# Two more expert weight units in the first round, and the first norm's g and b spread on chip

## What is computed

```python
x = _layer_norm(DEEPNORM_ALPHA * x + mixed, ln1_g[l], ln1_b[l])
ffn = _hier_moe(x, router_group_w[l], ..., expert_w_gate[l], expert_w_up[l], expert_w_down[l])
x = _layer_norm(DEEPNORM_ALPHA * x + ffn, ln2_g[l], ln2_b[l])
```

```python
def _hier_moe(x, wg_r, bg_r, we_r, be_r, w_gate, w_up, w_down):
    ...
    h = jax.nn.silu(jnp.einsum('td,edf->etf', xt, w_gate)) * jnp.einsum('td,edf->etf', xt, w_up)
    h = h * combine.T[:, :, None].astype(h.dtype)
    return jnp.einsum('etf,efd->td', h, w_down).reshape(B, S, D)
```

## Time and profile before

| what | us |
| --- | --- |
| median of 3 runs | 1340.41 |
| lowest and highest run | 1337.76, 1341.34 |
| the profiled execution, its own time | 1338.06 |
| its span (first to last instruction) | 1335.7 |
| PE busy in the span | 1308.4 |
| DVE, ACT busy | 584.3, 483.6 |

### The profile page before, as it was taken

The page is one execution under the profiler, slowest core; times in us unless marked ns, Lnnn a source line. Parts: engine busy times, 40 slices in busy tenths (PEclk is TensorE's granted clock), DMA queues, the critical chain, the costliest instruction groups (busy, mean ns, idle before and its releaser), DMA issues.

```text
span 1335.7 us, 17769 instructions
## 1 busy us (share of the span) xinstructions
PE 1308.4 (98%) x7293; PEld 962.3 (72%) x7293; DVE 584.3 (44%) x757; ACT 483.6 (36%) x671; POOL 28.2 (2%) x49
## 2 busy tenths in 40 slices
PE   9999999999999999999999999999999999999995
PEld 8999989998888888888888888854454443544442
DVE  4387444546545555554455555525112121221207
ACT  4554344435465634454333433422121121211211
POOL 1000000400000000000100001000000000000000
PEclk9999999999999999999999999999999999999997
DMA  9767555545545445654556795799999999999995
GB/s 304 266 197 260 171 189 190 189 159 174 172 136 179 157 142 173 198 163 162 183 197 212 267 391 182 264 398 414 421 421 422 421 421 421 422 420 421 421 407 222
DMA packets 120749, 364.95 MB, mean 273 GB/s; under 512 B 11560, under 2 KB 17128, under 8 KB 96880
## 3 DMA queue, kind: packets, MB, share of 16 engines
q1 hardware_dynamic: 114368, 359.58, 72.6%
q10 hardware_dynamic: 6320, 4.49, 1.1%
HBM read 361.95 MB, written 2.10 MB: 273 GB/s over the span
## 4 chain that ended last, share of the span: by engine, by line
PE 91%; DMA 6%; DVE 1%; SPq 1%; issue 0%; ACT 0%; DVEq 0%
PE main L1142 19%; PE main L1144 19%; PE main L1143 19%; PE main L541 14%; PE att L614 7%; PE att L495 4%; DMA mraw<-in_expert_w_down_dram 3%; DMA mraw<-in_expert_w_up_dram 2%; PE att L1391 1%; SPq L396 1%; PE main L507 1%; PE main L508 1%; PE att L1374 1%; PE att L1410 1%; PE att L1406 1%; PE att L1361 0%
## 5 line engine op out<-in xcount | busy, mean ns | idle before, releaser
L1808 DVE TENSOR_TENSOR wlo<-raw,whi 128x2048 fp32r<-128x2048 f32 x134 | 308.1, 2299 | 352.7 <-ACT whi L1557 352.7
L1557 ACT ACTIVATE whi<-raw 128x2048 fp32r<-128x2048 f32 x134 | 256.1, 1911 | 412.0 <-PE main L1144 409.8
L541 PE MATMUL main<-mraw,xg 128*64 128x512 f32 x1024 | 225.2, 595 | 0.7 <-DMA mraw<-in_expert_w_up_dram 0.6
L1142 PE MATMUL main<-whi,xhi 128*128 128x512 f32 (+1 forms) x544 | 203.8, 375 | 0.0
L1144 PE MATMUL main<-whi,xlo 128*128 128x512 f32 (+1 forms) x544 | 201.7, 371 | 0.0
L1143 PE MATMUL main<-wlo,xhi 128*128 128x512 f32 (+1 forms) x544 | 201.5, 370 | 0.0
L541 PEld LDWEIGHTS main<-mraw,xg 128*64 128x64 f32 x1024 | 72.0, 137 | 136.6 <-issue 135.4
L1142 PE MATMUL main<-xhi,whi 128*128 128x256 f32 (+1 forms) x560 | 159.5, 285 | 1.0 <-DVE wlo L1940 1.0
L1143 PE MATMUL main<-xlo,whi 128*128 128x256 f32 (+1 forms) x560 | 158.4, 283 | 0.0
L1144 PE MATMUL main<-xhi,wlo 128*128 128x256 f32 (+1 forms) x560 | 158.4, 283 | 0.0
L1144 PEld LDWEIGHTS main<-whi,xlo 128*128 128x128 f32 x544 | 102.5, 188 | 17.7
(11 more groups left out here) (331 smaller groups left out, 1336.5 us busy)
## 6 DMA issues: line engine op xcount, KB each, us to landing
raw<-in_w_in_dram SPq DMA_DIRECT2D x95, 1024.0 KB, 5.1
mraw<-in_expert_w_gate_dram SPq DMA_DIRECT2D x64, 1024.0 KB, 21.5
mraw<-in_expert_w_up_dram SPq DMA_DIRECT2D x64, 1024.0 KB, 22.9
mraw<-in_expert_w_down_dram SPq DMA_DIRECT2D x62, 1024.0 KB, 21.3
raw<-in_w_branch_dram SPq DMA_DIRECT2D x24, 1024.0 KB, 5.1
raw<-in_w_out_dram SPq DMA_DIRECT2D x16, 1024.0 KB, 6.7
xin<-in_x_dram SPq DMA_DIRECT2D x4, 512.0 KB, 8.2
mraw<-in_expert_w_down_dram SPq DMA_DIRECT2D x4, 512.0 KB, 6.9
```

What stands on the lines that cost most here:

```text
L541: ins = pe.matmul(main[0][half, w, :], xg[:, k, half], src[:, kk * DE:(kk + 1) * DE], start=(k == 0), stop=(k == KT - 1))
L1142: pe.matmul(o, ah, bh, start=start, stop=False, skip_group_check=skip)
L1557: act.activation(whi[:, u % SPLIT, 0:n], raw[:, slot, 0:n], ACT.Copy).then_inc(hi_done, 1)
L1808: dve.tensor_tensor(wlo[:, u % SPLIT, 0:n], raw[:, slot, 0:n], whi[:, u % SPLIT, 0:n].bitcast(F32), ALU.subtract).then_inc(lo_done, 1)
```

## The change

**Places.** Places 20 and 21 (over `khT` and `qst`) become first places: `NP` is 22. A list `first` gives the place of each of the first 22 units: units 0 to 5 in places 0 to 5, units 6 and 7 in places 20 and 21, units 8 and 9 in places 14 and 15 (those under `out_acc`), and units 10 to 21 in the rest in order. The ring of 19 begins at unit 22. The load of units 6 and 7 is issued where `l1g` and `l1b` were loaded. Units 22 and 23 are the ones in halves.

**g and b.** `l1g` and `l1b` are gone. The 8 rows are loaded into the first 8 partitions of a new tile `rows` (128 x 512), which POOL sets to zero at the start; ACT scales them by ALPHA in place after their transposition. PE spreads a row over all partitions with a matmul of f32, 128 x 512, whose stationary operand is a column of the identity (`spread`, four for g, into the four banks of `att`). For b the spread opens the accumulation of each of the 8 scatter pieces of pair 0 (`with_b`).

**Order.** `start_sum` on DVE stands ahead of `gated`, and is eight products of `xr` with `att`. PE waits for `acc_ok` ahead of pair 0's down product; SP no longer does.

```diff
         places.append(made["sig"])
+        norm_places = (len(places), len(places) + 1)
+        places += [made["khT"], made["qst"]]
         NP = len(places)
-        places += [made["khT"], made["qst"]]
+        late = [once[0], once[1]]
+        first = [0, 1, 2, 3, 4, 5, *norm_places, *late, *(j for j in range(6, router_place + 1) if j not in late)]
         mraw = [at(f"mraw{j}", o, [P, UNIT]) for j, o in enumerate(places)]
-        second_round = [j for j in range(NP) if j not in once]
-        GROWN = NP + len(second_round)
-        ring = second_round[:4] + [NP, NP + 1] + second_round[4:]
+        ring = [j for j in first if j not in once]
         assert len(ring) == MRAW
 
         def place(g):
-            if g < NP:
-                return g
-            return second_round[g - NP] if g < GROWN else ring[(g - GROWN) % MRAW]
+            return first[g] if g < NP else ring[(g - NP) % MRAW]
 
         def user_before(g):
-            return max((e for e in range(g) if place(e) == place(g)), default=None)
-
-        LOOP0, LAST0 = (FIRST * MU - GROWN) % MRAW, (FIRST * MU + MU - GROWN) % MRAW
+            return max((e for e in range(g) if place(e) == place(g)))
+
+        LOOP0, LAST0 = (FIRST * MU - NP) % MRAW, (FIRST * MU + MU - NP) % MRAW
         L2R = MU - MRAW
         l2g, l2b, ysb = (at(n, places[ring[(LAST0 + L2R + j) % MRAW]], [P, D]) for j, n in enumerate(("l2g", "l2b", "ysb")))
...
@@ -400,21 +399,21 @@
             sp.dma_start(mraw[j][:, cols].unsqueeze(1), expert_unit(g % MU, g // MU)[:, :, cols]).then_inc(mlanded[j], 16)
 
         def first_units(sp, some):
-            for r in some:
-                if r < 4:
+            for j in some:
+                if j < 4:
                     sp.wait_ge(unit_used, U1)
-                elif r < 6:
+                elif j < 6:
...
                     sp.wait_ge(r_ps, T)
-                else:
-                    sp.wait_ge(unit_used, U1 + 4 * QUADS - (1 if r < 8 + RAW else 0))
-                load_unit(sp, r, 0, r)
+                elif j < router_place:
+                    sp.wait_ge(unit_used, U1 + 4 * QUADS - (1 if j < 8 + RAW else 0))
+                load_unit(sp, first.index(j), 0, j)
 
         def moe_loads(sp):
-            first_units(sp, range(6, NP))
...
@@ -422,10 +421,7 @@
                 sp.wait_ge(m_used, user_before(g) + 1)
                 load_half(sp, g, 1)
             for g in range(NP + 2, FIRST * MU):
-                if user_before(g) is None:
-                    sp.wait_ge(acc_ok, 1)
-                else:
-                    sp.wait_ge(m_used, user_before(g) + 1)
+                sp.wait_ge(m_used, user_before(g) + 1)
                 load_unit(sp, g % MU, g // MU, place(g))
             sp.wait_ge(np_ok, 1)
             turns = sp.value_load(runs[0:1, 0:1], min_val=1, max_val=1 + PAIRS * (PASSES - 1))
...
@@ -496,16 +492,22 @@
                                         start=(k % 4 == 0 and t == 0), stop=(t == 1), skip_group_check=True)
                 ins.then_inc(xg_ps, 1)
 
-            def scatter(c, before):
+            def spread(o, r):
+                return pe.matmul(o, ident[:, r:r + 1].to_broadcast([P, P]), rows[:], start=True,
+                                 stop=(r < QUADS), skip_group_check=True)
+
+            def scatter(c, before, with_b=False):
 
                 pe.wait_ge(y_lo, before * 4 + c + 1)
                 for t in range(T):
                     n = 2 * c + t
                     if n >= 2:
                         pe.wait_ge(sc_free, before * 8 + n)
-                    rows, o = wsl[:, t * P:(t + 1) * P], scattered(n)
-                    pe.matmul(o, rows, yhi[:, c % 2, :], start=True, stop=False)
-                    pe.matmul(o, rows, ylo[:, c % 2, :], start=False, stop=True).then_inc(sc_ps, 1)
+                    place_t, o = wsl[:, t * P:(t + 1) * P], scattered(n)
+                    if with_b:
+                        spread(o, QUADS + c)
+                    pe.matmul(o, place_t, yhi[:, c % 2, :], start=not with_b, stop=False, skip_group_check=with_b)
+                    pe.matmul(o, place_t, ylo[:, c % 2, :], start=False, stop=True, skip_group_check=with_b).then_inc(sc_ps, 1)
 
             def last_scatter(d, m):
 
...
@@ -530,6 +532,11 @@
 
                     pe.wait_ge(xg_out, 1 + q + m * 4)
                     for w in range(2):
+                        if fixed == 0 and q == 2 and w == 1:
+                            pe.wait_ge(xg_out, 4)
+                            pe.wait_ge(gb_out, 2)
+                            for r in range(QUADS):
+                                spread(att[:, r, :], r).then_inc(l1_in, 1)
                         for a in range(2):
                             _, landed_, value = unit(4 * q + 2 * w + a)
                             pe.wait_ge(landed_, value)
...
@@ -547,7 +554,7 @@
 
                 def put(c):
                     if fixed != 0:
-                        scatter(c, m - 1)
+                        scatter(c, m - 1, fixed == 1)
 
                 pe.wait_ge(hot_ok, 1 + m)
                 put(0)
@@ -602,6 +609,8 @@
                 for f in range(DE // P):
                     if f % 2 == 0:
                         pe.wait_ge(ht_out, 1 + f // 2 + m * 2)
+                    if fixed == 0 and f == 0:
+                        pe.wait_ge(acc_ok, 1)
                     for a in range(2):
                         _, landed_, value = unit(4 * QUADS + 2 * f + a)
                         pe.wait_ge(landed_, value)
...
@@ -859,29 +868,26 @@
                 dve.tensor_scalar(bag[:, :, 1], bag[:, :, 1], EPS, None, ALU.add).then_inc(l2_var, 1)
 
             def start_sum():
-                dve.wait_ge(m_used, once[1] + 1)
-                dve.wait_ge(l1_in, 32)
+                dve.wait_ge(m_used, first.index(late[1]) + 1)
                 dve.wait_ge(z_ok, T)
-                for t in range(T):
-                    for q in range(QUADS):
-                        cols = slice(q * 512, (q + 1) * 512)
-                        ins = dve.scalar_tensor_tensor(out_acc[:, t, cols].rearrange("p (m k) -> p m k", k=4),
-                                                       xr[:, t, cols].rearrange("p (k m) -> p m k", k=4), ALPHA,
-                                                       l1g[:, cols].rearrange("p (m k) -> p m k", k=4), ALU.mult, ALU.mult)
-                link(ins)
-                for t in range(T):
-                    ins = dve.scalar_tensor_tensor(out_acc[:, t, :], l1b[:], ALPHA, out_acc[:, t, :], ALU.mult, ALU.add)
+                for q in range(QUADS):
+                    cols = slice(q * 512, (q + 1) * 512)
+                    dve.wait_ge(l1_in, q + 1)
+                    for t in range(T):
+                        ins = dve.tensor_tensor(out_acc[:, t, cols].rearrange("p (m k) -> p m k", k=4),
+                                                xr[:, t, cols].rearrange("p (k m) -> p m k", k=4),
+                                                att[:, q, :].rearrange("p (m k) -> p m k", k=4), ALU.mult)
                 ins.then_inc(acc_ok, 1)
                 dve.wait_ge(acc_ok, 1)
 
-            def pair_step(m, first=False):
+            def pair_step(m, starts=False):
                 dve.wait_ge(ws_t, 1 + m)
                 slots((m + 1) % PAIRS, m + 2)
                 slot_weights((m + 1) % PAIRS, m + 2)
+                if starts:
+                    start_sum()
                 gated(m)
-                if first:
-                    start_sum()
-                else:
+                if not starts:
                     put_last(m - 1)
                 put(m)
 
...
@@ -1022,6 +1030,7 @@
                         load(u, u % RAW, src.rearrange("(k p) n -> p k n", p=P), 4, 512,
                              turn=u - RAW + 1 + i * UB)
             sp.wait_ge(att_free, 9)
+            sp.wait_ge(consts, N_CONST)
             for j, name in enumerate(("ln1_g", "ln1_b")):
                 sp.dma_start(gb[j * QUADS:(j + 1) * QUADS, :], A[name][0].rearrange("(q n) -> q n", n=512)).then_inc(gb_in, 16)
             for dst, name in ((wrg, "router_group_w"), (wre, "router_expert_w")):
@@ -1029,8 +1038,7 @@
                              A[name][0].rearrange("(q p k) n -> p q (k n)", p=P, k=4)).then_inc(wr_in, 16)
             sp.dma_start(br[:, 0:NG], A["router_group_b"].to_broadcast([P, NG])).then_inc(br_in, 16)
             sp.dma_start(br[:, NG:NG + NE], A["router_expert_b"].to_broadcast([P, NE])).then_inc(br_in, 16)
-            sp.dma_start(l1g[:], A["ln1_g"].to_broadcast([P, D])).then_inc(l1_in, 16)
-            sp.dma_start(l1b[:], A["ln1_b"].to_broadcast([P, D])).then_inc(l1_in, 16)
+            first_units(sp, norm_places)
             for c in range(4):
                 for q in range(QUADS):
                     u = U1 + c * QUADS + q
...
@@ -1074,7 +1082,7 @@
             pool.affine_select(out=rowok[:], in_=rowok[:], compare_op=ALU.is_ge, fill=0.0, base=1 - CMP,
```

(31 more changed lines are left out.)

## The result

The changed kernel takes 1344.70 us in the median of 6 runs (1343.82 to 1346.59), against 1340.01 for the kernel before in 6 runs beside it. The ratio is 1.0039 with a 95% interval of 1.0028 to 1.0049: slower, by about 5 us. The forecast was 1340.3 and no difference, range 1337.0 to 1343.8; the measured time lies outside it. Rival (c), a spread at 0.85 us and 1344.9 in all, is the nearest. The profiled execution took 1345.38 us. Two executions far from all others are left out of the medians: one of the kernel before (5153.42 us) and one of the experiment with g's spreads later (2244.17 us, granted clock 0.56).

The account below looks back on a forecast made before the run. The stream of expert units bounds the kernel, with PE close behind. From the profiled 1338.06 us, minus 4.5 gain plus 4.4 for later use of unit 24 gives 1338.0, or 1340.3 on the median's scale; range 1337.0 to 1343.8.

Parts of the forecast that it names:

- Rival (c): PE's added f32 spreads cost 0.85 us each, making PE 4.5 us late: 1344.9 us in all; chance 6%.
- twelve spreads of 0.44 us: Price of the added f32 128 x 512 matmuls on PE, read from nearest trace rows: 0.44 us each, 5.3 in all.
- what PE has more: Part pricing PE's added matmuls in pairs 0 and 1; ten of them make unit 24 used 4.4 us later.
- Unit 24 and the slack of 4.5 us: Unit 43's load waits for PE to use unit 24; its 4.5 us of slack caps the gain from two more places.
- The restart: A unit loaded into an empty queue, such as unit 43, lands 4.8 us after issue.
- The first hole: Units 30 and 31 wait for units 10 and 11; the stream stands still some 3 us, which does not decide.
- PE's own path: PE gets 5.3 us longer, but its 5.7 us of waits for the stream take that up.
- Work that costs nothing: Sum's start on DVE (5.5 to 8.8 us), later units 8 and 9, and ACT's and POOL's additions all stay hidden.
- (d): DVE's start of the sum comes late, holding PE and the stream; at 2.0 us a product, 1344.8 us; chance 4%.
- (e): Units 6 and 7 go out early but the stream, limited by `m_used`, is never ahead: 1340.4 to 1342 us; chance 3%.
- (a): Restarting the dry load stream costs up to 2.4 us more than taken: 1342.7 us; chance 12%.

## Why the prediction was wrong

**The step that failed** is the term "twelve spreads of 0.44 us" in the part on what PE has more. On PE's path they measured 3.80 us for the four of g (3.63 in their own chain row, 0.91 each) and 6.75 for the eight of b (0.84 each), 10.55 in all instead of 5.3. The reading of the nearest rows was wrong in two ways, and both could be seen in the document. First, the eight matmuls of the earlier trace rows (L1490) are transposes through the identity, which the program calls `pe.transpose`, and not products. Second, an f32 product is two rows of the trace: the program's order lists a gather as eight matmuls (`x8`), and the chain shows sixteen for it. The gather's row of the kernel before:

```profile
880.74 1.98 PE att L495 x16
```

So 1.98 us for sixteen rows is 0.25 us for a product of 128 columns, and 1.07 us for four rows of 256 columns is two products, 1.07 us for 512 columns. The expert products were misread in the same way: their 64 rows in 13.93 us are 32 matmuls of the program (eight units with four each, `gate_up`), so two that share the array take 0.87 us, not 0.44. I had counted the rows of the trace as if they were the program's. The count should have been made in the one place where both views show the same instruction.

The Trainium skill's page FP8 and Floating Point Precision (TensorE Precision Notes) says four passes for true FP32. The run bears it out: 0.86 us for a spread's two rows in the chain, at a granted clock of 1.00, is 4 x 512 columns at 2.4 GHz (0.853). The stationary operand's step of zero, the other reason that rival (c) named, is not needed for it: the gather's products have none and take 0.22 to 0.25 us for 128 columns, and the fp32r spreads have it and take 0.28. The prediction set the page against a row that was of another kind of instruction, and gave its case 6%.

**Unit 24 and the slack of 4.5 us: right in mechanism.** With the measured price unit 24 is late by 3.8 + 5.2 = 9.0 us (from 58.6 to 67.6 us behind the first product), less 4.5 is 4.5, and unit 43 landed 4.5 us later (72.45 against 67.96). The restart took 4.9 us, where 4.8 was read from the earlier trace rows. The rest of the loss at the last landing (5.8 us in the profiles), 1.3 us, arises behind unit 43. Pauses of the stream of over 0.3 us each add up to 2.7 us there, 2.1 in the kernel before, so they cover about half; what makes them stays open.

**The first hole: size off.** Forecast about 3 us; it was 6.0. The spreads of g took 3.8 instead of 1.8, and the restart there took 6.1 us from issue to landing, as in the earlier trace rows and not as in the earlier trace rows. In the run without b the same load, issued 29.45 us behind the first product as here, took 4.9, so 6.1 does not belong to that place. It was right that it does not decide while unit 24 is this late; in the version without spreads it takes 2.9 of the 5.0 us.

**PE's own path.** Its slack was 7.0 us where I took 5.7, its load 10.6 where I took 5.3: it would have cost 3.5 us by itself. So either limit alone would have made the change slower. With unit 24 late by 9.0 us the prediction's sum is 1338.06 - 4.5 + 9.0 + 2.35 = 1344.9, by the wait for unit 24. Rival (c) reached its 1344.9 by PE's own path, 10.2 - 5.7 = 4.5 us, and put the stream at 4.0. The runs show the two the other way round (3.5 and 4.5), so its price was right and its time right by luck.

**Work that costs nothing: right.** The products of `start_sum` took 0.97 us each (7.75 for eight), and ended at 906.1, well ahead of `hh` at 911.8. Units 8 and 9, issued later than before, were waited for by nobody. ACT's and POOL's additions show in no wait. Rivals (d) and (e) did not occur, and (a) only in the first hole.

## What to carry to other kernels

Price an added matmul by an instruction of the same kind, type and shape, and check on one of them how many rows of the trace one instruction of the program makes. When a stream of loads and an engine run nearly level, look for the loads that wait for that engine and work out their slack. Here unit 43 had 4.5 us of it, less than the 5.0 that two buffers more should give, and with the 9.0 us of spreads ahead of unit 24 it landed 4.5 us later than before. Work that must be added goes behind the releases that the stream waits for, into the steps where the engine waits anyway.

## What the runs showed that I had not expected

- An f32 spread of 128 x 512 takes 0.84 to 0.91 us and two rows of the trace, the same in fp32r 0.23 to 0.28 us and one; in fp32r a stationary operand that repeats one column costs nothing beyond (the spreads among the scatter's matmuls have their pace).
- A load of 1 MB into a queue just run dry took 4.9 us from issue to landing at one place (unit 43, at 942.55) and 6.1 at another (unit 30, at 904.41). The latter load took 4.9 in the runs without b and with b in pair 5. Issued with 2.1 to 2.4 us of the queue left, it took 7.5 us in the run without spreads, 7.3 with the late f32 spreads and 5.5 with the late fp32r ones. What makes the difference is open; it is what rival (a) feared.
- Two places more were worth 2.3 us (0.9982, 0.9973 to 0.9991) at best, where the carried bytes say 5.0.
- With the new places every profile loses a little more at two points. From unit 43's landing to the last one it is 371.9 to 373.1 us in the seven with the new places, 371.3 and 371.4 in the two with the old. The last piece of the output lands 2.5 to 3.2 us behind DVE's last instruction, with the old places 2.1. No run tests what makes either.
